# A transformer layer pair on one core: weight slots dealt out by which comes free first

## The reference

```python
def reference(x, positions, ..., c_2, w_ada_2, b_ada_2, ...):
    x = first_block(x, positions, ...)
    return second_block(x, c_2, w_ada_2, ...)

# first block
h = h + concatenate([y_mla, y_swa]) @ w_out
m = rms_norm(h, mlp_norm)
h = h + square(relu(m @ w_up)) @ w_down
# second block
mod = silu(c) @ w_ada + b_ada          # 2048 x 12288, one row of c
sh1, sc1, g1, sh2, sc2, g2 = split(mod, 6)
z = (x * (1 + sc1) + sh1) @ w_in + b_in
...
mix = (gate_a * y_a + gate_b * y_b) @ w_o + b_o
x = layer_norm(ALPHA * x + g1 * mix, ln1_g, ln1_b)
f = square(relu((x * (1 + sc2) + sh2) @ w_m1 + b_m1)) @ w_m2 + b_m2
x = layer_norm(ALPHA * x + g2 * f, ln2_g, ln2_b)
```

## Time and profile before

| what | us |
|---|---|
| median of three runs | 2429.3 (2428.83 to 2429.86) |
| the profiled execution | 2428.6 |
| its span | 2426.8 |
| TensorE busy | 2376.5 (98% of the span) |
| VectorE busy | 1710.0 (70%) |
| ScalarE busy | 1049.4 (43%) |

### The profile page before, as it was taken

How to read it: one execution, slowest core, us unless ns; L and a number is a source line. 1 busy time by engine, 2 the same in 40 slices (tenths; PEclk the granted TensorE clock), 3 DMA queues, 4 the chain that set the end, 5 groups by cost and what they waited for, 6 DMA issues and landing times.

```text
span 2426.8 us, 30941 instructions
## 1 busy us (share of the span) xinstructions
PE 2376.5 (98%) x13376; PEld 2051.0 (85%) x13376; DVE 1710.0 (70%) x1559; ACT 1049.4 (43%) x999; POOL 29.8 (1%) x61
## 2 busy tenths in 40 slices
PE   7999999999999999989999999999999999999998
PEld 7998888888778888878888888997888888888887
DVE  7777577878777777765677666787764566774665
ACT  5464544434334334455645443343543443443443
POOL 0000000000000000000000000000000000000000
PEclk9999999999999999999999999999999999999999
DMA  7334477777777787775545547875455557775553
GB/s 274 134 130 151 174 262 287 288 290 271 280 294 278 296 309 285 299 268 189 211 162 181 184 177 269 299 278 200 173 190 197 186 190 301 273 278 211 186 193 110
DMA packets 79816, 558.73 MB, mean 230 GB/s; under 512 B 9034, under 2 KB 11285, under 8 KB 13248
## 3 DMA queue, kind: packets, MB, share of 16 engines
q1 hardware_dynamic: 74832, 528.25, 58.9%
q0 software_dynamic: 4848, 28.50, 3.3%
HBM read 547.26 MB, written 9.45 MB: 229 GB/s over the span
## 4 chain that ended last, share of the span: by engine, by line
PE 90%; DVE 4%; DMA 3%; ACT 2%; issue 1%; SPq 0%; ACTq 0%; DVEq 0%
PE ps L582 27%; PE ps L585 13%; PE ps L613 12%; PE ps L615 12%; PE ps L614 12%; DMA stage<-wstream 3%; PE ps L550 2%; PE ps L551 2%; PE ps L552 2%; DVE w_lo L1509 2%; ACT w_hi L1055 1%; PE ps L580 1%; PE ps L625 1%; PE ps L627 1%; PE ps L626 1%
## 5 line engine op out<-in xcount | busy, mean ns | idle before, releaser
L1509 DVE TENSOR_TENSOR w_lo<-stage,w_hi 128x2048 fp32r<-128x2048 f32 x402 | 918.4, 2288 | 459.0 <-ACT w_hi L1055 455.1
L1055 ACT ACTIVATE w_hi<-stage 128x2048 fp32r<-128x2048 f32 x402 | 766.6, 1911 | 755.1 <-DMA stage<-wstream 402.8
L582 PE MATMUL ps<-xs,w_hi 128*128 128x512 f32 x3200 | 998.5, 397 | 16.1 <-DVE w_lo L1509 14.0
L585 PEld LDWEIGHTS ps<-xs,w_lo 128*128 128x128 f32 x3000 | 564.9, 188 | 132.0
L585 PE MATMUL ps<-xs,w_lo 128*128 128x256 f32 x3000 | 591.6, 279 | 0.0
L582 PEld LDWEIGHTS ps<-xs,w_hi 128*128 128x128 f32 x3200 | 495.7, 189 | 31.2 <-DVE w_lo L1509 17.6
L613 PE MATMUL ps<-w_hi,hs 128*128 128x512 f32 x1008 | 394.4, 391 | 0.0
L615 PE MATMUL ps<-w_lo,hs 128*128 128x512 f32 x1008 | 392.7, 390 | 0.0
L614 PE MATMUL ps<-w_hi,hs 128*128 128x512 f32 x1008 | 392.6, 389 | 0.0
L613 PEld LDWEIGHTS ps<-w_hi,hs 128*128 128x128 f32 x1008 | 189.3, 188 | 41.7 <-issue 2.2
L614 PEld LDWEIGHTS ps<-w_hi,hs 128*128 128x128 f32 x1008 | 189.3, 188 | 39.7 <-issue 0.7
(11 more groups left out here) (414 smaller groups left out, 2248.2 us busy)
## 6 DMA issues: line engine op xcount, KB each, us to landing
stage<-wstream SPq DMA_DIRECT2D x497, 1024.0 KB, 4.9
spectra<-k_made POOLq DMA_DIRECT2D x4, 1024.0 KB, 7.7
k_spec<-spectra POOLq DMA_DIRECT2D x4, 1024.0 KB, 6.4
xraw<-xT SPq DMA_DIRECT2D x4, 512.0 KB, 11.4
resid<-x SPq DMA_DIRECT2D x2, 1024.0 KB, 15.7
w<-w POOLq DMA_DIRECT2D x16, 128.0 KB, 5.9
parked<-resid POOLq DMA_DIRECT2D x1, 2048.0 KB, 7.4
resid<-parked POOLq DMA_DIRECT2D x1, 2048.0 KB, 9.0
```

Of the source, the lines that this page charges most:

```text
L582: mm = pe.matmul(out[c], hi[c], rhs[:, k, :], start=(first and j == 0), stop=end)
L585: mm = pe.matmul(out[c][:, S:2 * S], lo[c], rhs[:, k, 0:S], start=False, stop=False)
L1055: act.activation(w_hi[:, w % HIGH, 0:m], stage[:, n % RING, 0:m], ACT.Copy).then_inc(hi_ready, 1)
L1509: tt(w_lo[:, slot, 0:m], stage[:, slot, 0:m], f(w_hi[:, w % HIGH, 0:m]), ALU.subtract).then_inc(lo_ready, 1)
```

## The change

A planner `slots()` walks through `ORDER` once when the program is built. It keeps for each of the five slots the time, in units of w tiles, at which it expects it to be free, and gives each item the slot with the lowest. A w tile k is taken to free its slot at k + 1.0, an ada tile behind w tile k at k - 1.1. SP's load then waits for the item that held that slot, and the engines wait for the slot's count of uses.

```diff
+def slots():
+
+    free, uses = [-1.0 + i / RING for i in range(RING)], [0] * RING
+    held, k = [None] * RING, 0
+    slot, use, held_by = [], [], []
+    for n, (kind, i) in enumerate(ORDER):
+        k = i if kind == "w" else k
+        s = min(range(RING), key=lambda j: free[j])
+        uses[s] += 1
+        slot.append(s)
+        use.append(uses[s])
+        held_by.append(held[s])
+        held[s] = n
+        free[s] = k + 1.0 if kind == "w" else k - 1.1
+    return slot, use, held_by
+
+
+SLOT, USE, HELD_BY = slots()
...
-            sp.dma_start(stage[:, n % RING, 0:m], ws[n][:, 0:m]).then_inc(loaded[n % RING], 16)
+            sp.dma_start(stage[:, SLOT[n], 0:m], ws[n][:, 0:m]).then_inc(loaded[SLOT[n]], 16)
...
-            kind, k = ORDER[n - RING]
+            kind, k = ORDER[HELD_BY[n]]
...
-            act.wait_ge(loaded[n % RING], 16 * (n // RING + 1))
+            act.wait_ge(loaded[SLOT[n]], 16 * USE[n])
...
-                dve.wait_ge(loaded[n % RING], 16 * (n // RING + 1))
-                src = stage[:, n % RING, :]
+                dve.wait_ge(loaded[SLOT[n]], 16 * USE[n])
+                src = stage[:, SLOT[n], :]
```

More of the change, by code:

```diff
@@ L548, in weights_moved @@
                     o2 = acc(u)[:, c]
-                    hi, lo = w_hi[:, w % HIGH, a:a + P], w_lo[:, place(w) % RING, a:a + P]
+                    hi, lo = w_hi[:, w % HIGH, a:a + P], w_lo[:, SLOT[place(w)], a:a + P]
                     pe.matmul(o2, hi, rhs[:, k, 0:S], start=(first and j == 0), stop=False)
@@ L559, in narrow @@
                 a = slice(k * ROPE, k * ROPE + ROPE)
-                hi, lo = w_hi[:, w % HIGH, a], w_lo[:, place(w) % RING, a]
+                hi, lo = w_hi[:, w % HIGH, a], w_lo[:, SLOT[place(w)], a]
                 pe.matmul(o2, hi, rhs[:, k, 0:S], start=(k == 0), stop=False)
@@ L576, in both_halves @@
                 hi = [w_hi[:, w % HIGH, (j * 2 + c) * P:(j * 2 + c) * P + P] for c in range(2)]
-                lo = [w_lo[:, place(w) % RING, (j * 2 + c) * P:(j * 2 + c) * P + P] for c in range(2)]
+                lo = [w_lo[:, SLOT[place(w)], (j * 2 + c) * P:(j * 2 + c) * P + P] for c in range(2)]
                 if end:
@@ L593, in tokens_apart @@
                     a = j * 512
-                    hi, lo = w_hi[:, w % HIGH, a:a + 512], w_lo[:, place(w) % RING, a:a + 512]
+                    hi, lo = w_hi[:, w % HIGH, a:a + 512], w_lo[:, SLOT[place(w)], a:a + 512]
                     o2 = ps[:, 2 * (u % 2) + t, :]
@@ L1054, in split @@
             m = columns_of(w)
-            act.activation(w_hi[:, w % HIGH, 0:m], stage[:, n % RING, 0:m], ACT.Copy).then_inc(hi_ready, 1)
+            act.activation(w_hi[:, w % HIGH, 0:m], stage[:, SLOT[n], 0:m], ACT.Copy).then_inc(hi_ready, 1)
         def square_block(n, u_end, last=False):
@@ L1504, in split @@
         def split(w):
-            slot = place(w) % RING
+            slot = SLOT[place(w)]
             dve.wait_ge(hi_ready, w + 1)
```

## The result

The changed kernel takes 2458.1 us (median of four runs, 2452.3 to 2460.2), the kernel before 2429.4 us beside it. The ratio is 1.0115, with an interval of 1.0096 to 1.0133: 28.7 us slower. The forecast was 2460 us. The profiled execution took 2460.2 us with a span of 2458.4, which is 31.6 us more than the span in the earlier trace rows.

The account below looks back on a forecast made before the run. TensorE, busy 98% of the span, was taken as the bound, so only its 50 us of standing still could change. Terms 20.6 + 0.4 + 1 + 8.5 = +30.5 us on 2428.6 gave a forecast of 2460 us, range 2424 to 2486.

Parts of the forecast that it names:

- The loop: Ada product, release, load of weight tile two behind, copy, subtraction, next product: 11.3 us against two TensorE tiles' 11.17 or 10.88.
- The landing: Time for a loop's load to land, taken as 5.2 us between the lowest, 4.7, and the median, 5.6.
- the links of 11.7 and 7.5: Product-to-product steps with a 5.2 us landing: 25 over two tiles at 11.7 us, 13 over one at 7.5.
- The waits of TensorE: Time the loop adds: +20.6 us in the first MLP's second half, +0.4 in its first, +1 at ada tiles 80 to 95.
- The second half of the first MLP: Ada tiles 31 to 69: +20.6 us, with TensorE's waits on the subtraction coming to 15 to 30 us.
- the first half: Ada tiles 0 to 31, first MLP: loop just fits; -2.6 us of waits gone, +3 for lost lead, so +0.4.
- The lead: Ada tiles 31 to 69 can begin 4.8 us further ahead and end without their 1.8 us lead: 6.6 us off.
- Ada tiles 70 to 79: Nine links of 11.7 us, 105.3 against 104.0 us now, inside the lead: 0.
- Ada tiles 80 to 95: 15 links of 11.7 us, 175.5 against 170.9 us now; 4.6 more, inside the lead but for about +1.
- The clock: TensorE drops to 1.2 GHz after long waits, 1.7 us lost each, at about five places: +8.5 us.
- the forecast's own range: 2432 us with landings of 4.8 us, to 2488 with the median 5.6 and eight falls of the clock.
- rival 1: Change works as built: weight loads go a tile earlier, first-MLP waits and slow clock go, 2416 us; chance 0.14.

Follow-up runs that it names:

- the half product: The changed kernel with each ada tile's product taken over 1024 of its 2048 columns; 2414.4 us, ratio 0.9933 to the kernel before.
- the best kernel: The changed kernel with the planner taking an ada tile to free its slot at k - 0.5, not k - 1.1; 2413.6 us, ratio 0.9930 to before.

## Why the prediction was right, point by point

**The loop.** Right. It is in the chain of waits with all its links, SP waits for the product at all 96 loads, and the time answers to the loop's length in both directions (43.7 us gone with 1.07 us less, 54.8 more with 0.7 more).

**The landing, 5.2 us, and so the links of 11.7 and 7.5.** Between the releases of the trace the 25 two-tile links of ada tiles 31 to 69 took 11.50 us in the mean and the 13 one-tile links 7.56; 25 x 11.50 + 13 x 7.56 = 385.8, where the forecast had 390.0. The landing was the term that was too large: the loads of these links landed in 4.9 us in the mean, and long ones were few, since such a load goes out first behind its release. With 4.9 in place of 4.78 the bare links of 11.3 and 7.1 are 11.4 and 7.2, and that leaves 0.1 and 0.35 us. The latter is VectorE's: in nine of the 13 one-tile links the product began within 0.03 us of the landing, in four it began 1.2 to 1.3 us later, behind a split (4 x 1.2 / 13 = 0.37).

**The waits of TensorE.** The forecast gave the loop 20.6 + 0.4 + 1 = 22.0 us. Measured are 18.9 us more of standing still, 17.4 of them for w_lo. The second half of the first MLP is right in place: 22.3 us of waits for w_lo from 690 to 1090 us, where the forecast said 15 to 30. In the first half I had let the 2.6 us of waits go; they rose to 5.4, one of 1.1 us at 446 us came new, and the stretch took 4.0 us more where I had said 0.4. The step that failed there is that the waits of before would go: the lead does not come up (3.1 us before and 2.2 us after in the mean of w tiles 45 to 105), since the loop just keeps pace, and what was late before is late still.

**The lead, -6.6 us.** This term failed, and the total hid it. I had let the stretch begin with more lead and end with none. The splits of w tiles 102 to 108 were 4.0 us ahead in the mean before and 3.7 after, and the last tile of the MLP had a lead of 2.2 us where it was 1.8. So nothing was taken from the links' 23.0 us (385.8 - 362.8): on TensorE the time from the end of w tile 105 to the end of w tile 169 grew by 23.7 us. In the other direction, those 23.7 us have TensorE's slow stretches in them, for which I had added 8.5 us by themselves. 23.0 - 6.6 + 8.5 is 24.9, near 23.7, because the two errors cancel. That is luck.

**Ada tiles 70 to 79: 0.** Wrong by some 4 us (from the seam behind the first MLP to the one ahead of the last it took 3.9 us longer). The links were 11.9 us and I had looked only at the lead of the splits. The late step was another: the evacuation `mixacc`, in VectorE's queue behind split and product. The chain of waits, 1535 to 1565 us:

```profile
1548.45 4.76 DMA stage<-wstream
...
1553.24 1.92 ACT w_hi L1075
...
1555.18 2.29 DVE w_lo L1529
1557.47 2.21 DVE stage L1839 x2
1559.68 0.61 DVE mixacc L2125
...
1560.42 0.36 PE ps L645
```

TensorE waited 2.2 us for it, and ran slow for 3.4 us behind it. I had named what is queued behind the waiting load on SP, and not what is queued behind the product on VectorE.

**Ada tiles 80 to 95: +1.** They took 0.5 us less than before, and the last MLP is as long as it was; there the loop fits.

**The clock: +8.5.** Near in size, partly by luck: in the first MLP there were four falls and not five, but two of them lasted twice as long. Nor does the length of a wait say whether the clock falls: waits of 2.58 us (until 552.8) and 2.15 us (until 1057.9) were followed by no fall, one of 1.86 us (until 1076.4) was. Rows by stretch (length, busy PE PEld DVE ACT POOL, PEclk, DMA share, GB/s), the fall behind the wait of 4.2 us and one of the long ones:

```profile
786.90:790.30 3.40, 3.40 (x13) 2.87 (x13) 3.40 (x2) 0.00 (x0) 0.00 (x0) 0.55 0.45 188
967.40:970.80 3.40, 2.09 (x6) 1.80 (x7) 2.69 (x2) 2.40 (x2) 0.00 (x0) 0.50 1.01 426
970.80:974.20 3.40, 3.40 (x12) 2.92 (x12) 3.40 (x4) 0.00 (x0) 0.00 (x0) 0.50 0.25 106
```

Half of the time at the lower level (1.2 GHz), summed over the run, is 18.7 us against 8.5 before. But TensorE stood still for a part of that time. Of what it worked at the lower level half is 16.1 us, against 7.6 before, so 8.5 us more were lost: 8.9 against 1.6 in the first MLP, 1.7 in the fall at 1561 us, and 0.5 less at the seams and the end. The other 4.2 us of the 12.7 by which TensorE's busy time grew are not traced.

**The sum.** 22.0 + 8.5 = 30.5 forecast, 31.6 by the profiled executions, 28.7 by the medians. The terms' errors are 3 to 9 us each and of both signs, so that the total came within 2 us is in part luck. The mechanism, the loop and its place in the first MLP, is not. The upper end of the forecast's own range adds up to 2487, not 2488.

**The rivals.** That the change works as intended did not come true, and the reason lies where the forecast put it: with a link 1.1 us shorter it does (the half product gives 2414.4, and rival 1 had 2416). The forecast also set the fit of the Trainium skill ("DMA: Bandwidth & Descriptors", section "Anatomy of one DMA"), 4.4 us for a tile's load, against the rows. The section gives it for DMAs that GpSimd issues, and these are issued by SP, so it was no measure of this load; the loads of the loop took 4.76 to 4.94 us in the rows above. And with 4.4 us the loop would be 4.4 + 1.93 + 2.29 + 2.21 + 0.05 = 10.88 us, an estimate, which is below the up pair's 11.17 but only level with the tok pair's 10.88, not below both.

## What to carry to other kernels

When slots or buffers are dealt out by who is free first, write down for each slot the whole way from its release back to its next release, and compare its length with the time that the bounding engine takes for as many steps as it spans. Here a way of 11.3 us over steps of 11.17 us kept the lead down and cost 44.5 us beside the best kernel, and with one step more of distance the same way cost 2.6 us (2416.2 against 2413.6). The best kernel gave a reused slot to the item whose chain behind the load is shortest (the next ada tile, load and product), not to one whose chain goes through ScalarE and VectorE first. A constant of the planner that differs by 0.6 of a step (k - 1.1 for k - 0.5) turned a gain of 0.7% into a loss of 1.2%; when a planner is changed, try its constants on both sides.

## What the runs showed of the hardware

The loads behind one release land one by one. Behind the release at 760.7 us three went out at 760.75, 761.12 and 761.60 and landed at 765.62, 768.10 and 770.59: 4.9 us for the first and 2.48 us more for each further one, which is 1 MiB at 423 GB/s. A stretch in which the DMA engines were busy throughout (share 1.02) shows the same rate (last column, GB/s):

```profile
793.40:797.00 3.60, 3.60 (x24) 3.16 (x23) 2.29 (x1) 2.49 (x2) 0.00 (x0) 1.00 1.02 423
```

So a longer median to landing, 7.0 us against 5.6, says here that more loads stand far back in a burst. Of the loads from 458 to 1080 us none went out as the third of a burst before and 33 did after, with a median of 9.0 us; 58 were the second in both, at 7.0 us in both. The first of a burst is no slower than before (median 4.87 us, before 4.84), and that is the one that counts in a loop. By the Trainium skill (the page and section named above, for DMAs issued by GpSimd) the slope would be 1 MiB over 436 GB/s, an estimated 2.4 us, near the 2.48 us of the trace; the fixed part came out at 4.9 - 2.5 = 2.4 us for these loads of SP, where the section has 2.0.

I had not expected the lower clock to hold for 6.8 us after some waits: behind the one that ended at 968 us it was 0.50 for the 6.8 us shown above, and behind the longer one of 4.2 us that ended at 785.6 only for 3.4 us. The two falls of 6.8 us in the first MLP began at 844.6 and 967.4 us, 1.4 and 1.3 us before TensorE went on; the one of 3.4 us began at 786.5, 0.9 us after it had gone on.
